# Differential attention in a ten-stage block: values first, queries and keys by pairs of heads, the softmax between the product chunks, a third split buffer

## The reference, cut to what matters

```
def _diff_attention(x, w_qkv, w_o, lam_p, subln_g, rel_table, lambda_init):
    q, k, v = split(x @ w_qkv, 3)            # 8 heads; q, k: 2 parts of 64 each; v: 128
    lam = exp(sum(lp[0]*lp[1])) - exp(sum(lp[2]*lp[3])) + lambda_init
    for each block of 128 queries, with its keys 0..kend:
        s = q . k * 64**-0.5 + bias(rel), masked causal        # for both parts
        p = softmax(s)
        a = p[part 0] - lam * p[part 1]
        out = a @ v
    o = out * rsqrt(mean(out**2) + 1e-5) * subln_g * (1 - lambda_init)      # per head
    return o @ w_o
x = layernorm(ALPHA_2 * x + _diff_attention(x, ...))
```

## Time and profile before

| what | value |
|---|---|
| median of 3 runs | 1816.81 us (1814.79 to 1818.55) |
| profiled execution | span 1816.1 us from first to last instruction; its own time isn't given apart |
| attention, first product to last | 1473.4 to 1608.8 us |
| head loop | 1547.0 to 1579.6 us |

### The profile page before, as it was taken

The page is one execution under the profiler, slowest core; times in us unless marked ns, Lnnn a source line. Parts: engine busy times, 40 slices in busy tenths (PEclk is TensorE's granted clock), DMA queues, the critical chain, the costliest instruction groups (busy, mean ns, idle before and its releaser), DMA issues.

```text
span 1816.1 us, 21082 instructions
## 1 busy us (share of the span) xinstructions
PE 1417.9 (78%) x8842; PEld 918.0 (51%) x8842; DVE 600.7 (33%) x978; ACT 427.8 (24%) x661; POOL 39.4 (2%) x47
## 2 busy tenths in 40 slices
PE   7999775575665689986754656557999999799997
PEld 6787221121121275661211212115999988589997
DVE  5554000000000257640000000003555555755556
ACT  3443000000000243420000000002443444644443
POOL 3000000000000002100000000000000000000000
PEclk9988878787697799998878868879999999799999
DMA  9736999999999932569999999998465754035560
GB/s 339 219 127 236 409 424 424 423 424 424 424 425 424 393 133 96 206 248 424 424 423 424 424 424 424 424 424 309 149 198 185 241 180 136 24 116 186 180 210 25
DMA packets 146659, 533.47 MB, mean 294 GB/s; under 512 B 9740, under 2 KB 73500, under 8 KB 97308
## 3 DMA queue, kind: packets, MB, share of 16 engines
q1 hardware_dynamic: 143972, 527.07, 74.0%
q10 hardware_dynamic: 1176, 2.18, 0.8%
q0 software_dynamic: 1440, 3.18, 0.6%
HBM read 529.78 MB, written 2.62 MB: 293 GB/s over the span
## 4 chain that ended last, share of the span: by engine, by line
PE 49%; DMA 38%; DVE 6%; SPq 4%; ACT 2%; issue 1%; POOL 0%; DVEq 0%; ACTq 0%; POOLq 0%
PE bank L1607 14%; PE bank L594 11%; DMA moe_slots<-in_moe_w_up 9%; DMA arena<-in_moe_w_up 7%; PE bank L1623 7%; DMA ring<-in_moe_w_down 6%; DMA ring<-in_moe_w_up 6%; DMA xT<-in_moe_w_down 4%; PE bank L1085 4%; DMA arena<-in_moe_w_down 3%; PE bank L1124 3%; PE bank L491 3%; SPq L1251 2%; SPq L1245 2%; PE bank L312 1%; DMA xT<-in_moe_w_up 1%
## 5 line engine op out<-in xcount | busy, mean ns | idle before, releaser
L558 DVE TENSOR_TENSOR w_lo<-ring,w_hi 128x1024 fp32r<-128x1024 f32 x210 | 256.6, 1225 | 271.1 <-ACT w_hi L553 264.0
L553 ACT ACTIVATE w_hi<-ring 128x1024 fp32r<-128x1024 f32 x210 | 221.7, 1059 | 347.4 <-PE bank L1607 151.2
L1085 PE MATMUL bank<-ring,arena 128*32 128x512 f32 x1016 | 211.7, 731 | 102.9 <-DMA ring<-in_moe_w_up 50.3
L1124 PE MATMUL bank<-ring,arena 128*32 128x512 f32 x536 | 147.2, 881 | 86.6 <-DMA moe_slots<-in_moe_w_down 26.7
L1607 PE MATMUL bank<-xT_hi,w_hi 128*128 128x256 f32 x704 | 199.8, 284 | 0.6 <-DVE xT_lo L454 0.4
L1607 PE MATMUL bank<-xT_hi,w_lo 128*128 128x256 f32 x704 | 199.2, 283 | 0.0
L1607 PE MATMUL bank<-xT_lo,w_hi 128*128 128x256 f32 x704 | 199.2, 283 | 0.0
L1218 DVE TENSOR_TENSOR arena<-arena,bank 64x512 f32<-64x512 f32 x32 | 22.1, 691 | 458.2 <-ACT arena L1158 458.2
L1085 PEld LDWEIGHTS bank<-ring,arena 128*32 128x32 f32 x1016 | 46.4, 122 | 227.8 <-issue 220.0
L1607 PEld LDWEIGHTS bank<-xT_hi,w_hi 128*128 128x128 f32 x704 | 135.1, 192 | 1.6 <-issue 0.9
L1607 PEld LDWEIGHTS bank<-xT_lo,w_hi 128*128 128x128 f32 x704 | 135.1, 192 | 0.7
(11 more groups left out here) (272 smaller groups left out, 2254.3 us busy)
## 6 DMA issues: line engine op xcount, KB each, us to landing
ring<-in_moe_w_gate SPq DMA_DIRECT2D x76, 1024.0 KB, 26.5
ring<-in_moe_w_down SPq DMA_DIRECT2D x67, 1024.0 KB, 27.1
ring<-in_moe_w_up SPq DMA_DIRECT2D x51, 1024.0 KB, 26.7
arena<-in_moe_w_up SPq DMA_DIRECT2D x28, 1024.0 KB, 26.9
arena<-in_moe_w_gate SPq DMA_DIRECT2D x28, 1024.0 KB, 26.5
moe_slots<-in_moe_w_up SPq DMA_DIRECT2D x24, 1024.0 KB, 27.1
moe_slots<-in_moe_w_gate SPq DMA_DIRECT2D x24, 1024.0 KB, 26.5
moe_slots<-in_moe_w_down SPq DMA_DIRECT2D x24, 1024.0 KB, 26.8
```

The source lines that it names most:

```text
L553: nc.scalar.activation(dst, raw, ACT.Copy).then_inc(hi_ready, 1)
L558: nc.vector.tensor_tensor(lo, raw, hi.bitcast(F32), ALU.subtract).then_inc(split_ready, 1)
L1085: last = nc.tensor.matmul(ps[B_GU[j % 2]][32 * c:32 * c + 32, :], xin[:, k, j * CAP:(j + 1) * CAP], w, start=(k == 0), stop=(k == KD - 1), ...
L1124: last = nc.tensor.matmul(ps[B_DN[c]][32 * j:32 * j + 32, :], hT[:, j // 2, at:at + CAP], slot(ud[j], 2)[:, f % 2, c * HALF:(c + 1) * HALF ...
```

## The change

Four things, all in the attention stage.

1. **A third split buffer.** Chunk c uses buffer c % 3, the third being `h_hi` and `h_lo`, which otherwise hold the feed-forward stages' hidden layer. `split_hi` of chunk c now waits for chunk c - 3.
2. **Another order of chunks.** Values first (chunks 0 to 7, whole chunks for two row blocks of x each), then by pair p of heads two chunks of queries and two of keys (8 + 4p to 11 + 4p, banks 0 and 1), then the output projection, whose unit b is now rows 2b and 2b + 1 of `w_o` at all 1024 columns (chunks 24 to 31), so that it needs only heads 2b and 2b + 1. The loads in `att_sync` follow.
3. **The heads between the chunks.** Each step of a pair's heads stands between two chunks of the next pair; pair 3's between chunks of the output projection. The transposition of a pair's heads (`transpose_heads`), its copy (`z_copy`) and split (`z_split`) follow pair by pair.
4. **Another norm.** `norm(h)` on ScalarE takes squares of the head from PSUM, a logarithm and an exponential (exp(-0.5 ln(mean + floor))) in place of square root and reciprocal, and works on the output before its division by the softmax sum, with the floor scaled by that sum squared (one more small VectorE instruction in `combine`). `outputs(h)` applies that scale, so L1941 and the last reciprocals go. One table with both functions is loaded at the start of `att_scalar`. The copy of the transposed weights moves from ScalarE to VectorE (`weights_T`). Weights use bank 2, head outputs bank 3 for all heads, where before two banks each alternated.

```diff
+            def buffer(self, c):
+                return c % 3
+            def free(self, c):
+                return self.at + (c - 1 if c < 2 else max(c - 2, 0))
...
+            att_mix.token_block(pe, 0, (4, 5), ("x", gen))
+            att_mix.token_block(pe, 1, (6, 7))
+            for c in head_chunks(0):
+                pair_chunk(c)
+            for p in range(3):
+                a, b = 2 * p, 2 * p + 1
+                q0, q1, k0, k1 = head_chunks(p + 1)
+                pair_chunk(q0)
+                scores(a)
+                if p:
+                    values(b - 2)
+                pair_chunk(q1)
+                scores(b)
+                if p:
+                    transpose_heads(p - 1)
+                pair_chunk(k0)
+                transpose_weights(a)
+                pair_chunk(k1)
+                values(a)
+                transpose_weights(b)
+            pe.wait_ge(amax_ready, 6)
             for i in range(NT):
                 residual(pe, i)
-            transpose_z(pe, 2)
...
+            scores(6)
+            values(5)
+            att_mix.out_chunk(pe, 24)
+            scores(7)
+            transpose_heads(2)
+            att_mix.out_chunk(pe, 25)
+            transpose_weights(6)
+            att_mix.out_chunk(pe, 26)
+            values(6)
+            transpose_weights(7)
+            att_mix.out_chunk(pe, 27)
+            values(7)
+            att_mix.out_chunk(pe, 28)
+            transpose_heads(3)
+            for c in range(29, 32):
+                att_mix.out_chunk(pe, c)
...
+            def norm(h):
...
+                act.wait_ge(ao_psum, h + 1)
+                b = h % 2
+                for i in range(NT):
+                    ins = nc.scalar.activation(small_sq[:, i, 0:P], ps[3][:, i * P:(i + 1) * P], ACT.Square,
+                                               accum_out=at_ss[:, b, i:i + 1])
+                ins.then_inc(asq_ready, 1)
+                act.wait_ge(asq_ready, h + 1)
+                for i in range(NT):
+                    ins = nc.scalar.activation(at_log[:, b, i:i + 1], at_ss[:, b, i:i + 1], ACT.Ln,
+                                               bias=at_floor[:, b, i:i + 1], scale=1.0 / V_DIM)
+                ins.then_inc(alog_ready, 1)
+                act.wait_ge(alog_ready, h + 1)
+                nc.scalar.activation(at_scale[:, b], at_log[:, b], ACT.Exp, scale=-0.5).then_inc(ao_act, 1)
...
+            nc.scalar.preload_act_table_set("natural_log_exp_and_others")
...
+            for p in range(3):
...
+                keys(p)
+                lo(n + 2)
+                if p:
+                    outputs(a - 2)
+                logits(a)
+                lo(n + 3)
+                if p:
+                    outputs(b - 2)
+                logits(b)
+                combine(a)
+                lo(n + 4)
+                weights_T(a)
+                combine(b)
+                lo(n + 5)
+                weights_T(b)
```

More of the change, by code:

```diff
@@ L1866, in att_scalar @@
[L1866 to L1881 removed]
+            hi(10, 11)
@@ new lines, in att_scalar @@
+            queries(0)
+            hi(12, 13)
+            for p in range(3):
+                a, b = 2 * p, 2 * p + 1
+                n = head_chunks(p + 1)[0]
+                hi(n + 2)
+                if p:
+                    norm(a - 2)
+                hi(n + 3)
+                if p:
+                    norm(b - 2)
+                exps(a)
+                if p:
+                    z_copy(p - 1)
+                hi(n + 4)
+                queries(p + 1)
+                exps(b)
+                hi(n + 5)
@@ L1917, in outputs, with z_split @@
                 ins.then_inc(ao_vec, 1)
+            def z_split(p):
+                dve.wait_ge(chunk_done, att_mix.done(23))
+                split_T_pair(dve, split_before("z", 2), p, at_zT, zT_act, 2 * KD)
+            lo(2, 3, 4, 5)
             v_half(0)
-            logits(0)
-            att_mix.lo(dve, 22)
-            logits(1)
-            att_mix.lo(dve, 23)
-            combine(0)
-            v_half(1)
-            att_mix.lo(dve, 24, 25)
-            for h in range(A_HEADS):
-                if h:
-                    combine(h)
-                if h + 2 < A_HEADS:
-                    logits(h + 2)
-                if h:
-                    outputs(h - 1)
@@ new lines, in att_vector @@
+            keys(3)
+            z_split(0)
+            outputs(4)
+            logits(6)
+            outputs(5)
+            lo(26)
+            z_split(1)
+            logits(7)
+            combine(6)
+            lo(27)
+            weights_T(6)
+            combine(7)
+            lo(28)
+            weights_T(7)
+            z_split(2)
+            outputs(6)
+            lo(29)
+            outputs(7)
+            lo(30)
+            z_split(3)
+            lo(31)
+        def att_sync(sp):
+            w_in, w_out = (w.rearrange("(k p) n -> p k n", p=P) for w in (a["w_qkv_2"][0], a["w_o_2"][0]))
+            parts = []
+            for b in range(2):
+                for half in range(2):
+                    parts.append(w_in[:, half * KD // 2:(half + 1) * KD // 2, 2 * D + b * HALF:2 * D + (b + 1) * HALF])
+            for p in range(4):
+                for at in (0, D):
+                    parts.append(w_in[:, :, at + p * 256:at + (p + 1) * 256])
+            for p in range(4):
+                parts.append(w_out[:, 2 * p:2 * p + 2, :])
+            for u, part in zip(att_u, parts):
+                wait_free(sp, u)
+                sp.dma_start(slot(u, part.shape[1]), part).then_inc(slot_landed[u.slot], 16)
```

252 lines of the change are left out of this document (132 added, 120 removed).

## The result

The change is faster: 1796.99 us median (1796.08 to 1799.73, 4 runs) against 1816.72 us (1814.79 to 1818.55, 4 runs), 19.7 us less, ratio 0.9887, 95% interval 0.9875 to 0.9898.

A forecast was written before the change was run, and what follows sets the result against it. TensorE bounds the products, a three-engine chain the head loop. TensorE's work with slow clock 115.3 us, waits 2.7 and switches 1 give a 119.0 us stage in place of 135.3: 1800.5 us in all, range 1797 to 1806.

The forecast's parts named there:

- the walk: Attention stage's engine queues followed in order at measured durations and assumed hand-overs, to find TensorE's waits: 2.7 us.
- the table load: ScalarE's square-root table loaded ahead of the layer norm behind the attention: 1.28 us long, cost 0 to 0.1 us.
- What it still waits for: TensorE's waits at transposed weights: 0.8 us at head 0, 0.3 each in pairs 1 and 2, 1.3 at head 6; 2.7 us.
- The residual: TensorE's residual piece in the attention stage, priced at 4.29 us from the old profile's row.
- Weights, values and heads: TensorE's pieces: transposed weights 0.47 us a head, values 0.85 us a head, heads' transpositions 1.9 us in all.
- The switches between kinds of matmul: TensorE going from small fp32 products to the chunks' and back, 29 pieces at 0.03 us each: 1 us.
- The bare chunks: TensorE's product chunks: 16 at 2.75 us and 16 at 2.88 us, 90.1 us.
- The slow clock: Lower TensorE clock in the stage's first chunk, following idle time ahead of the stage: 1.5 us kept in the sum.
- The chain shows through: Rival: every head, not four, waits 1.3 us for VectorE's combine, 10.4 us in place of 2.7; 1808 us; chance 0.12.
- The third buffer frees nothing: Rival: in-order ScalarE holds up the next split_hi, stage stays at 137 us; 1817 us, no change; chance 0.04.
- The table's drain: Rival: a ScalarE table switch ahead of the layer norm costs 1.3 us more than its row; 1801.8 us; chance 0.03.
- The clock falls among short pieces: Rival: TensorE's clock drops to 0.71 from chunk 13 to 28, 29 us more; 1829 us, slower; chance 0.05.

The follow-up runs named there:

- e4: The changed kernel unaltered, run again for a second profile: stage 114.7 us with the slow clock, 1795.88 us in all.
- e11: The changed kernel with combine ahead of the second logits, the same kernel as e6 run a second time: stage 111.8 us, 1793.52 us, ratio 0.9865.
- e9: The kernel of e6 plus 18 matmuls without use in TensorE's idle time ahead of the stage: stage 111.8 us, 1796.89 us, ratio 0.9882.
- e12: The kernel of e9 with 9 matmuls without use instead of 18: stage 111.85 us, median 1793.50 us, ratio 0.9864.
- e14: The kernel of e12 unaltered, profiled again for a third look at the first chunks: stage 111.85 us.
- e6: The changed kernel with combine(a) ahead of logits(b) on VectorE, likewise for heads 6 and 7: stage 113.4 us, 1796.36 us, ratio 0.9891.
- e1: The changed kernel with two split buffers in place of three: stage 139.6 us, 1820.22 us in all, ratio to before 1.0013.
- e5: The changed kernel with a pair's head pieces in one place behind the next pair's four chunks: stage 137.6 us, 1817.86 us, ratio 1.0003.

## Why the prediction was right or wrong

**The mechanism** held: TensorE's own work sets the stage, the two waits that the trace shows, at heads 0 and 6, are the largest of the walk and for what it named, split_hi and split_lo ended no wait, and the table load cost nothing. Of later walks, that for the table switches was near (124, measured 126.7 us); those for kernels with long waits were too low, 137 us for two buffers (139.6) and 131 to 135 for the heads together (137.6).

**The sum was too large, and the step that failed is the price of TensorE's pieces and waits.** Forecast were 119.0 us with 1.5 us of slow clock, so 117.5 without it; the first profile, without slow clock, measured 113.1, and e4, with it, 114.7. In the first profile:

- *What it still waits for, 2.7 us.* Measured 0.9 us of idle time, 0.29 at head 0 in place of 0.8 and 0.62 at head 6 in place of 1.3. At heads 2 and 4, 0.3 each in the walk, the trace shows no idle time; the chunk ahead of the weights takes 3.10 us there (1535.06 to 1538.16), where e11, with combine ahead, has 2.95. All of it together is worth 1.3 us, the difference between this stage and e11's 111.8. combine was taken as 1.4 us with its added instruction and takes 1.27 (1520.66 to 1521.93).
- *The residual, 4.29 us.* Measured 3.67 from its start to the next piece's. The row of before lay right behind the head loop, at a mean granted clock of 0.83 (1579.58 to 1583.87), and I carried its pitch into a stage that I forecast at full clock.
- *Weights, values and heads, 0.47 and 0.85 us a head and 1.9 in all.* From start to start the weights take 0.25 to 0.32, the values 0.58 to 0.69, the heads of a pair 0.36 to 0.42. With the scores, whose 0.86 was right, the pieces sum to 16.0 us where I had 19.4. In the earlier trace rows the weights stood ahead of scores, and so had part of the scores' start in their pitch: here a chunk ahead of scores takes 0.17 us more than a bare one, and 0.47 less 0.17 is 0.30. For the values I took a busy time less an overlap, not a pitch.
- *The switches between kinds of matmul, 1 us.* Too small, and this hid part of the rest. The chunks that have a piece behind them take 0.06 to 0.25 us more than bare ones (3.05 us ahead of scores, 2.94 ahead of values, where 2.88 is bare). Over the stage that is 2.5 us, idle time not counted.

Together: 1.8 + 0.6 + 3.4 less 1.5 = 4.3 us, of the 4.4 that lie between 117.5 and 113.1. The bare chunks came as forecast, 90.1 us.

**The slow clock, 1.5 us,** was right in size (1.6) and as the usual case; the first profile lacked it by luck: of the unaltered change's three profiles the other two have it. The reason that I gave for keeping it, the idle time ahead, is what e9 and e12 to e14 show.

**The range** ended at 1797.0 below, 3.5 us under the forecast. The bounds that the prediction itself names below (no waits, no slow clock, no price for switches) come to 2.7 + 1.5 + 1 = 5.2 us, 1795.3; I cut them to 3.5, as if not all could fall on one side, and had no bound at all for the residual and the pieces at full clock. The medians of few runs vary besides: 1793.5 and 1796.4 for one kernel (e11 and e6).

**The rivals.** The chain shows through: no, VectorE was busy for 37.16 of 44.70 us among the pairs, and that left room. The third buffer frees nothing: no; e1 shows what it would have cost, a stage of 139.6 us where I had 137. The table's drain: no, in two places. The clock falls among short pieces: no; the granted clock is 1.00 through all windows behind the first 5 us in the first profile and in e4, and the Trainium skill's rule on micro-idles (TensorE: Matmul & The Clock Gate, "A second HAM failure mode: psum-queue depth-cycling") does not show in waits of 0.3 and 0.6 us. Where waits of up to 4.7 us came back (e5), so did a clock of 0.89.

## What to carry to other kernels

In this kernel a chain over three engines in strict order could be hidden under matrix work only when the queues had room to run ahead: interleaving without the extra buffer, and the buffer without interleaving, each gave nothing, and both gave 20 us. Walk the queues for one turn; here it named who waits for whom, with waits that were 0.3 to 0.7 us too long. Take a piece's price at the clock it will run at, from start to start between the neighbours that it will have, and give the switch to and from it a row of its own.

## What the runs showed of the hardware

- A table switch of ScalarE costs its 1.28 us, and the next instruction starts 0.01 to 0.02 us behind it, ahead of a layer norm and in the midst of work.
- 2.36 us of idling at the end of a layer norm were followed, a microsecond or two into the next products, by a stretch at the lower clock that costs 1.6 us, in ten of twelve profiles. 2.2 us of matmuls without use in that gap prevented it in three profiles of three, and twice as many, which delayed the start, in one of one.
- Idle times of 0.29 and 0.62 us among 113 us of matmuls left the granted clock at 1.00; waits of up to 4.7 us (e5) came with 0.89.
- The stages ahead of the attention keep DMA busy for 0.84 of their time, and vary from run to run: the stage's first product lies between 1469.6 and 1477.4 us in the sixteen profiles. That is more than the order of combine (1.3 us) or the slow clock (1.6 us) is worth.
